# Row picks between the dense layers and the experts: merged branches laid out by token block, last ranks in the middle of the picks, loads and a store in another order

## The reference, cut to what matters

```python
merged = sigmoid(gate_a) * y_attn + sigmoid(gate_g) * y_gla     # T x D
h = h + (merged @ w_out) * valid
xn2 = rms_norm(h, norm2_w)
# hierarchical experts: best of 4 groups, then the best 2 of its 8 experts
y_ffn = hier_moe(xn2, router_group, router_expert, w_gate, w_up, w_down)
return h + y_ffn
```

## Time and profile before

| what | value |
|---|---|
| median of 3 runs | 678.75 us (676.87 to 681.87) |
| the profiled execution | 676.36 us, of which 674.5 us is the span from the first to the last instruction |
| busy share of the span | PE 97%, PEld 75%, DVE 58%, ACT 32%, POOL 15% |
| mean granted TensorE clock | 0.997 of full speed |
| experts (from 414.92 us on) | 38% of the span |

### The profile page before, as it was taken

How to read it: one execution, slowest core, us unless ns; L and a number is a source line. 1 busy time by engine, 2 the same in 40 slices (tenths; PEclk the granted TensorE clock), 3 DMA queues, 4 the chain that set the end, 5 groups by cost and what they waited for, 6 DMA issues and landing times.

```text
span 674.5 us, 11222 instructions
## 1 busy us (share of the span) xinstructions
PE 652.9 (97%) x4481; PEld 505.9 (75%) x4481; DVE 390.9 (58%) x736; ACT 216.2 (32%) x448; POOL 101.5 (15%) x138
## 2 busy tenths in 40 slices
PE   4999999999999999999999988999999999999998
PEld 2679999988888888888789987575757575656565
DVE  4648334778897878776663665453534435351515
ACT  5446222234434444432435455202020202110112
POOL 3300015999200000000000010110100101010010
PEclk9999999999999999999999999999999999999999
DMA  7442223202322211111554070999999999999973
GB/s 242 145 124 64 64 63 122 66 1 63 115 75 62 63 64 63 63 63 63 161 201 168 34 279 17 399 415 415 412 417 412 419 410 419 410 418 411 418 282 125
DMA packets 49798, 138.78 MB, mean 206 GB/s; under 512 B 6202, under 2 KB 28235, under 8 KB 41556
## 3 DMA queue, kind: packets, MB, share of 16 engines
q1 hardware_dynamic: 47298, 134.37, 52.3%
q0 software_dynamic: 2304, 3.64, 1.5%
q10 hardware_dynamic: 146, 0.07, 0.0%
HBM read 138.62 MB, written 4.19 MB: 212 GB/s over the span
## 4 chain that ended last, share of the span: by engine, by line
PE 87%; DVE 6%; ACT 4%; issue 2%; DMA 1%; POOL 0%; ACTq 0%; DVEq 0%
PE bank L960 17%; PE bank L603 12%; PE bank L604 12%; PE bank L605 12%; PE bank L973 8%; PE bank L1083 8%; PE bank L819 1%; DVE y_lo L1869 1%; PE bank L912 1%; PE bank L984 1%; PE bank L846 1%; PE bank L843 1%; PE bank L611 1%; ACT whi L1202 1%; DVE sig_a L1584 1%
## 5 line engine op out<-in xcount | busy, mean ns | idle before, releaser
L1515 DVE TENSOR_TENSOR wlo<-wraw,whi 128x2048 fp32r<-128x2048 f32 (+1 forms) x25 | 56.5, 2258 | 20.0 <-ACT whi L1202 20.0
L603 PE MATMUL bank<-xhi,whi 128*128 128x512 f32 x160 | 64.5, 403 | 0.0
L603 PE MATMUL bank<-whi,xhi 128*128 128x256 f32 x224 | 64.5, 288 | 0.0
L604 PE MATMUL bank<-xlo,whi 128*128 128x512 f32 x160 | 63.3, 396 | 0.0
L604 PE MATMUL bank<-wlo,xhi 128*128 128x256 f32 x224 | 63.0, 281 | 0.0
L605 PE MATMUL bank<-whi,xlo 128*128 128x256 f32 x224 | 62.9, 281 | 0.0
L605 PE MATMUL bank<-xhi,wlo 128*128 128x512 f32 x160 | 62.9, 393 | 0.0
L960 PE MATMUL bank<-wgate,xgT 128*64 128x256 f32 x512 | 58.4, 381 | 0.7 <-ACT xgT L1392 0.7
L960 PE MATMUL bank<-wup,xgT 128*64 128x256 f32 x512 | 58.4, 381 | 0.0
L973 PE MATMUL bank<-wdown,hT 128*64 128x512 f32 x256 | 58.1, 595 | 0.0
L1846 DVE SCALAR_TENSOR_TENSOR hg<-bank,pair_w,hs 128x256 f32<-128x256 f32 x16 | 7.7, 484 | 81.1 <-ACT hs L1420 81.1
(11 more groups left out here) (327 smaller groups left out, 1355.6 us busy)
## 6 DMA issues: line engine op xcount, KB each, us to landing
wgate<-in_expert_w_gate SPq DMA_DIRECT2D x32, 1024.0 KB, 13.8
wup<-in_expert_w_up SPq DMA_DIRECT2D x32, 1024.0 KB, 16.5
wdown<-in_expert_w_down SPq DMA_DIRECT2D x32, 1024.0 KB, 21.8
wraw<-in_w_in SPq DMA_DIRECT2D x17, 1024.0 KB, 5.5
wraw<-in_w_out SPq DMA_DIRECT2D x4, 1024.0 KB, 5.2
h<-in_x SPq DMA_DIRECT2D x4, 512.0 KB, 5.1
wraw<-in_w_gla_branch SPq DMA_DIRECT2D x2, 1024.0 KB, 5.0
wraw<-in_w_attn_branch SPq DMA_DIRECT2D x2, 1024.0 KB, 5.1
```

The lines of the kernel that those rows point to most:

```text
L603: nc.tensor.matmul(ps, lhi(k), rhi(k), start=(k == 0), stop=False)
L604: nc.tensor.matmul(ps, lhi(k), rlo(k), start=False, stop=False)
L1515: nc.vector.tensor_tensor(wl, raw, wh.bitcast(F32), ALU.subtract).then_inc(s_lo, 1)
```

## The change

`mhi` and `mlo` become `[P, NB, KT, P]`, block first, so that the 1024 values of a block and a partition lie in one run. `rowhi` and `rowlo` now read `h` in its own order and write one run; the step of 8 elements moves to the stationary operand of `select`. The merge (L1247, L1586) writes four pieces of 128 instead of one of 512; the products with `w_out` read 128 contiguous columns as before. `rowhi` and `rowlo` come one unit earlier in the list. `select` is split by part, and `rowhi`, `route`, `rank`, `pick`, `rowlo` of block 3 stand after the third of eight half selects. `weigh` 2 on DVE moves behind the copies of `xgT`, beside `weigh` 3. SP loads the three down weights before it stores the rows of block 3.

```diff
-        s += [("rowhi", (n - 6) // 4)] if n >= 6 and n % 4 == 2 else []
-        s += [("rowlo", (n - 7) // 4)] if n >= 7 and n % 4 == 3 else []
+        s += [("rowhi", (n - 5) // 4)] if n >= 5 and n % 4 == 1 else []
+        s += [("rowlo", (n - 6) // 4)] if n >= 6 and n % 4 == 2 else []
...
     s += [("rank", 2), ("hT", 15), ("pick", 2), ("rstd", 3), ("logit", 14), ("logit", 15)]
-    s += [("select", b) for b in range(3)] + [("route", 3), ("rowhi", 3), ("rank", 3), ("pick", 3), ("rowlo", 3), ("select", 3)]
+    s += [("select", 0, 0), ("select", 0, 1), ("select", 1, 0), ("rowhi", 3), ("route", 3), ("rank", 3), ("pick", 3), ("rowlo", 3)]
+    s += [("select", 1, 1), ("select", 2, 0), ("select", 2, 1), ("select", 3, 0), ("select", 3, 1)]
...
-        mhi = at("mhi", 48 * K1, [P, KT, T], F32R)
-        mlo = at("mlo", 64 * K1, [P, KT, T], F32R)
+        mhi = at("mhi", 48 * K1, [P, NB, KT, P], F32R)
+        mlo = at("mlo", 64 * K1, [P, NB, KT, P], F32R)
...
+        def rows_of(t, b):
+
+            return t[:, b, :, :].rearrange("p k c -> p (k c)")
...
-                    b = step[1]
-                    if b == 0:
+                    _, b, part = step
+                    if b == 0 and part == 0:
                         for k in PICK_BANKS:
                             pe.wait_ge(banks.free[k], banks.uses[k])
-                    for part, t in enumerate((mhi, mlo)):
-                        pe.wait_ge(s_rowlo if part else s_rowhi, b + 1)
-                        pe.wait_ge(s_ohr, b + 1)
-                        for g in range(4):
-                            for j in range(2):
-                                last = nc.tensor.matmul(tiles[PICK_BANKS[g]][:, j * 2 * P:(j + 1) * 2 * P],
-                                                        t[:, 2 * g + j, b * P:(b + 1) * P], onehot_r[:, b, :],
...
+                    pe.wait_ge(s_rowlo if part else s_rowhi, b + 1)
+                    pe.wait_ge(s_ohr, b + 1)
+                    for g in range(4):
+                        for j in range(2):
+                            rows = rows_of(mlo if part else mhi, b)[:, 2 * g + j:D:KT]
+                            last = nc.tensor.matmul(tiles[PICK_BANKS[g]][:, j * 2 * P:(j + 1) * 2 * P], rows, onehot_r[:, b, :],
...
             load(1, 1, True)
-            store_rows(NB - 1)
             sp.wait_ge(s_pick[3], 1)
             sp.wait_ge(s_cast, 2)
             load(0, 0, False, (1,))
             load(1, 1, False)
+            store_rows(NB - 1)
...
-                        nc.scalar.activation(mhi[:, j, :], sig_a[:, j, :], ACT.Copy).then_inc(s_mhi, 1)
+                        nc.scalar.activation(mhi[:, :, j, :], by_block(sig_a[:, j, :]), ACT.Copy).then_inc(s_mhi, 1)
...
-                    nc.scalar.activation(mhi[:, :, b * P:(b + 1) * P], by_chunk(b), ACT.Copy,
+                    nc.scalar.activation(rows_of(mhi, b), h[:, b, :], ACT.Copy,
                                          scale=b1[:, b, 5:6]).then_inc(s_rowhi, 1)
...
                 elif kind == "weigh":
-                    weigh(step[1])
+                    if step[1] < NB - 2:
+                        weigh(step[1])
...
-                    nc.vector.scalar_tensor_tensor(mlo[:, :, cb], by_chunk(b), b1[:, b, 5:6], mhi[:, :, cb].bitcast(F32),
+                    nc.vector.scalar_tensor_tensor(rows_of(mlo, b), h[:, b, :], b1[:, b, 5:6], rows_of(mhi, b).bitcast(F32),
                                                    ALU.mult, ALU.subtract).then_inc(s_rowlo, 1)
...
                 last.then_inc(s_xgT[2 * s], 1)
+            weigh(NB - 2)
             weigh(NB - 1)
```

More of the change, by code:

```diff
@@ L542, in split, with by_block @@
             return own if c == 0 else w_view(t[split_buffer(c)], c)
-        def by_chunk(b):
-            return h[:, b, :].rearrange("p (c k) -> p k c", k=KT)
+        def by_block(t):
+            return t.rearrange("p (b t) -> p b t", b=NB)
+        def rows_of(t, b):
+            return t[:, b, :, :].rearrange("p k c -> p (k c)")
         def q_heads(b, g):
@@ L618, in cols, with tokens @@
                 return lambda k: t[:, k, a:b]
+            def tokens(t, b):
+                return lambda k: t[:, b, k, :]
             def first_outputs():
@@ L630, in first_outputs @@
                             pe.wait_ge(s_mhi, k + 1)
-                            nc.tensor.matmul(ps[:, 0:CW], mhi[:, k, 0:P], wh[:, k, :], start=(k == 0), stop=False)
-                            nc.tensor.matmul(ps[:, 0:CW], mhi[:, k, 0:P], wl[:, k, :], start=False, stop=False)
+                            nc.tensor.matmul(ps[:, 0:CW], mhi[:, 0, k, :], wh[:, k, :], start=(k == 0), stop=False)
+                            nc.tensor.matmul(ps[:, 0:CW], mhi[:, 0, k, :], wl[:, k, :], start=False, stop=False)
                     for i, (ps, wh, wl) in enumerate(pair):
@@ L635, in first_outputs @@
                             pe.wait_ge(s_mlo, k + 1)
-                            last = nc.tensor.matmul(ps[:, 0:CW], mlo[:, k, 0:P], wh[:, k, :], start=False, stop=(k == KT - 1))
+                            last = nc.tensor.matmul(ps[:, 0:CW], mlo[:, 0, k, :], wh[:, k, :], start=False, stop=(k == KT - 1))
                         if ks[-1] == KT - 1:
@@ L710, in _ @@
                         ps = banks.take(pe, "unit", step)
-                        last = mm3(ps[:, 0:n], cols(mhi, u * P, (u + 1) * P), cols(mlo, u * P, (u + 1) * P),
+                        last = mm3(ps[:, 0:n], tokens(mhi, u), tokens(mlo, u),
                                    cols(wh, 0, n), cols(wl, 0, n), KT)
@@ L901, in _ @@
                 elif kind == "select":
-                    b = step[1]
-                    if b == 0:
+                    _, b, part = step
+                    if b == 0 and part == 0:
                         for k in PICK_BANKS:
                             pe.wait_ge(banks.free[k], banks.uses[k])
-                    for part, t in enumerate((mhi, mlo)):
-                        pe.wait_ge(s_rowlo if part else s_rowhi, b + 1)
-                        pe.wait_ge(s_ohr, b + 1)
-                        for g in range(4):
-                            for j in range(2):
-                                last = nc.tensor.matmul(tiles[PICK_BANKS[g]][:, j * 2 * P:(j + 1) * 2 * P],
-                                                        t[:, 2 * g + j, b * P:(b + 1) * P], onehot_r[:, b, :],
-                                                        start=(b == 0 and part == 0 and j == 0), stop=(b == NB - 1 and part == 1 and j == 1))
-                            if b == NB - 1 and part == 1:
-                                last.then_inc(s_pick[g], 1)
+                    pe.wait_ge(s_rowlo if part else s_rowhi, b + 1)
[4 more added lines that the diff above has]
+                            last = nc.tensor.matmul(tiles[PICK_BANKS[g]][:, j * 2 * P:(j + 1) * 2 * P], rows, onehot_r[:, b, :],
+                                                    start=(b == 0 and part == 0 and j == 0), stop=(b == NB - 1 and part == 1 and j == 1))
+                        if b == NB - 1 and part == 1:
+                            last.then_inc(s_pick[g], 1)
             def oh(s, b):
@@ L1585, in _ @@
                             dve.wait_ge(s_mhi, j + 1)
-                            nc.vector.tensor_tensor(mlo[:, j, :], t, mhi[:, j, :].bitcast(F32), ALU.subtract).then_inc(s_mlo, 1)
+                            nc.vector.tensor_tensor(mlo[:, :, j, :], by_block(t), mhi[:, :, j, :].bitcast(F32), ALU.subtract).then_inc(s_mlo, 1)
                     elif name == "wo":
@@ L1779, in _ @@
                     dve.wait_ge(s_rowhi, b + 1)
-                    cb = slice(b * P, (b + 1) * P)
-                    nc.vector.scalar_tensor_tensor(mlo[:, :, cb], by_chunk(b), b1[:, b, 5:6], mhi[:, :, cb].bitcast(F32),
+                    nc.vector.scalar_tensor_tensor(rows_of(mlo, b), h[:, b, :], b1[:, b, 5:6], rows_of(mhi, b).bitcast(F32),
                                                    ALU.mult, ALU.subtract).then_inc(s_rowlo, 1)
```

## The result

| kernel | median, us | runs | ratio to the kernel before, 95% interval |
|---|---|---|---|
| before | 677.27 | 16 | |
| changed | 681.43 | 16 | 1.0056 (1.004 to 1.0072) |

The change makes the kernel 0.56% slower, about 3.8 us by the ratio (4.2 between the medians). Forecast were 673.7 us, 5.0 less than 678.75, the median of three runs of the kernel before; the 16 runs here put that kernel at 677.27. The profiled execution of the changed kernel has a span of 679.5 us, 5.0 more than before.

The account below looks back on a forecast made before the run. PE was taken to bound the kernel, with its weak stretch before the experts. The order saves 5.0 us, the step, weighing and SP's order cost 0: 678.75 - 5.0 = 673.7 us, range 671.3 to 680.3.

Parts of the forecast that it names:

- The bound and the order: PE bounds; reordering picks and ranks around the selects moves the first expert product from 414.92 to 409.93, 5.0 us.
- The standstill of the earlier trace: PE idle about 2 us before hT 15, until 400.54; claimed to go, and by assumption the clock's fall with it.
- The splits: rowhi on ACT and rowlo on DVE, read and written in one run, fall to 1.05 and 1.28 us.
- The deferred weighing: weigh 2 and 3 behind DVE's copies: info ready at +5.94, PE there at +5.99 us, cost 0, at most 2.0.
- The stationary operand with a step: 64 fp32r select loads on PE with columns 32 bytes apart: taken as no extra cost, 0.119 us per product.
- p: Spacing in us between select products on PE, forecast 0.119.
- 402.15 + 64p: Start of the first expert product on PE's sum, p being the spacing of the 64 select products in us.
- The first rival: At the selects the step costs, spacing 0.22 us: first expert product at 416.2, total 680.0 us; chance 0.15.
- SP's order: Three down weights before block 3's store: cost 0, only a tail of 3 MB in front, late gathers harmless.
- Sum: Whole kernel: 5.0 us less than 678.75, giving 673.7 us, 0.74% less.
- The range: Whole kernel: 671.3 to 680.3 us, from PE's least sum less scatter up to the first rival.

Follow-up runs that it names:

- e4_run_loads_store: Changed kernel with the selects' stationary operands in one run and block 3's store again before the down weights: 674.53 us, ratio 0.9925 to the kernel before.
- e2_store_last: Kernel before with only SP's order changed, three down weights loaded before block 3's rows are stored: 680.29 us, ratio 1.0015.
- e3_run_loads: Changed kernel with the selects' stationary operands in one run again, the store still behind the down weights: 673.3 us, ratio 0.9918 to the kernel before.
- e8_weigh_early: e4_run_loads_store with block 2's weighing moved on DVE to just behind the remainder of block 3: 672.34 us, ratio 0.9929 to the kernel before.
- e11_e4_again: e4_run_loads_store run once more, unchanged: 671.96 us, ratio 0.9926 to the kernel before.
- e5_step2: Changed kernel with the store before the down weights and rows stored in runs of two, so select operands have step 2: 673.0 us, ratio 0.9933.
- e9_turned_step: e4_run_loads_store with the step of 8 put on the turned loads of gathered rows, ACT writing scaled rows in one run: 672.0 us, ratio 0.992.
- e7_layout_alone: Kernel before with only the new layout, short splits and stepped select operands; order and SP's queue untouched: 682.77 us, ratio 1.0072.
- e10_store_last_again: e3_run_loads run once more, unchanged: 673.18 us, ratio 0.9944 to the kernel before.

## Why the prediction was wrong

**The bound and the order: right.** The chain, link by link, gave 409.93 for the first expert product. With the step and the late store taken out (e4_run_loads_store) it is 410.15, and 409.85 in the second take; the time is 0.75% below the kernel before, where 5.0 us were forecast. The standstill of the earlier trace rows went, and none of the ten profiled executions in the new order, that of the changed kernel among them, shows a fall of the clock between 398 and 415.

The 5.0 us are two things, though. From the last product of rank 2 to the first expert product it is 16.50 us in the kernel before, 14.92 in e2_store_last, which has the same order but no fall of the clock there, and 11.4 to 11.6 in the new order without the step (e3_run_loads, e4_run_loads_store and their repeats). So 3.4 to 3.5 us come from the order itself and 1.6 from a fall that the profiled execution of before happened to have; the prediction took its going with the standstill as an assumption. How many executions of the kernel before have that fall isn't on record.

**The splits: right in the main.** L1388 (`rowhi`) took 1142 ns on the median and L1788 (`rowlo`) 1277 ns, against 1.05 and 1.28 us. Neither is on PE's path.

**The deferred weighing: a little off.** Forecast were 0 us with 0.05 to spare. In e4_run_loads_store `info` was ready 5.92 us after the last group's start (forecast 5.94), but PE had come 5.90 us after it (forecast 5.99), and it stands 0.42 us before L930. This is most of what its way from the first expert product to the end is longer than before (260.1 against 259.6 us). In the changed kernel PE waits for nothing there: its last group takes 1 us longer while DVE's copies start after the group's first products, so `info` is ready 6.33 us after the group's start and PE comes at 6.64. Moving it (e8_weigh_early) gained nothing.

**The stationary operand with a step: the term that failed.** The prediction took p = 0.119 us, with 0.22 as the upper bound, because stepped turned loads were 0.108 to 0.115 us apart and fp32r loads in a run 0.113 us. It read both as one rate of delivery, a column in 0.84 ns, that an fp32r load would not exceed. The runs show instead that the cost of the step goes by the kind of load: a step of 32 bytes adds 52 ns to a turned load of 141 ns and 150 ns to an fp32r load of 188 ns, and of the first 5 ns reach the distance between two products, of the second 123. Whether the 0.108 us of L662 has the price of its step in it already can't be said, as no row has it without the step. The prediction's estimate of 107 ns for a load of 128 columns fits the spacing of fp32r loads in one run, and not with the step of 8. The real p is 0.242 us; 64 x 0.123 = 7.9 us, and the formula of the prediction, 402.15 + 64p, gives 417.6, measured 417.83, of which 0.4 us is a later end of the dense stage. The first rival had the side right, that the step costs, with a chance of 0.15. No run shows its p of 0.22; the runs showed 0.234 at a step of 4 and 0.242 at 8. The splits' own rows, doubled by the same step, were the better neighbours than rows of PE with another kind of load.

**SP's order: the other term that failed.** Forecast 0, measured 2.0 us (681.43 less 679.39, and 261.6 less 259.8 us of span behind the first expert product). Two sentences failed. The first is that the store finds at most the tail of the 3 MB in front: it was issued 6.2 us behind the weights, as reckoned, but these filled the DMA engines only from about 419 on, and it landed 3.9 us later than with a free queue. The second is that a late gather for body 1 has most of a body to spare. It doesn't: before the change the second gather took 10.5 us from its issue to its landing, at 437.7, and the eight transposes that read it started at 439.7, 2.0 us later. A delay of 3.9 us of the store used all that up and 1.6 us of PE. The early weights brought nothing back; no reader of them had been waiting.

**Sum.** 5.0 won by the order and the clock (first L967 5.1 us earlier in e11_e4_again), 7.9 lost to the step, 2.0 to the store: +4.9 us, where the profiled spans show +5.0 (679.5 less 674.5) and the ratio of the runs +3.8. Most of what is between has a place. The profiled execution of before took 676.36 us, 0.9 less than the median of 677.27, and that of the changed kernel 681.29, 0.1 less than its median. A part of this, 0.4 us, shows already at the end of the dense stage (398.79 against 398.42 for the same rank product). Medians of one kernel moved by 2.6 us from one set of runs to the next (674.53 and 671.96 for e4_run_loads_store). The range, 671.3 to 680.3, missed 681.43, because it summed the step at 0.22 and the store at 0. That it came so near is luck in part: its base of 678.75 was 1.5 us above the median of 16 runs, and the same sum from 677.27 ends at 678.8.

The versions without the two failed parts beat both kernels: e4_run_loads_store, e5_step2 and e9_turned_step all lie 0.7 to 0.8% under the kernel before.

## What to carry to other kernels

When a step can't be avoided, it belongs where it is hidden: on a split under another engine's work, or on turned loads, and not on plain fp32r stationary operands that follow each other with 256 moving columns. Storing runs of two (step 2) gives both sides nearly all of their speed: loads of 194 instead of 188 ns, 1.27 us of ACT instead of 1.14, and 1.7 us of DVE in four pieces instead of 1.28 in one. A row of another kind of the same instruction is no bound: the same step reached the spacing with 5 ns in one kind and 123 ns in the other. Before a store is put behind loads on one queue, follow it to its last reader: here store, gather and transposes were one chain with 2 us of slack. And when a saving contains a fall of the clock, price it apart: it was 1.6 of 5.0 us here, and of three executions with a standstill at this place one did not have it.

## What the runs showed of the hardware

Fp32r stationary loads of 128 columns at the upper clock took 188 ns in one run, 194 ns at a step of 8 bytes, 330 ns at 16 and 338 ns at 32; products of 256 columns that follow each other were 0.113 to 0.119, 0.120, 0.234 and 0.242 us apart. Turned fp32 loads took 141 ns in one run and 193 ns at 32 bytes; a group of 16 with its matmuls took 1.97 and 2.05 us. Stepped fp32r products at the granted clock 0.50 were 0.24 us apart, as at 1.00; those in one run were 0.23 and 0.12. ACT wrote 1024 values in 2.25 us reading with a step of 32 bytes, in 1.14 us from a run. A 512 KB store issued 6.2 us after three loads of 1 MB on the same queue landed 6.99 us after its issue, and 3.1 us after it with none in front. Behind standstills of PE of 1.85 us (kernel before), 0.72 us (e7_layout_alone) and 1.76 us (e2_store_last, at 442) the granted clock was at 0.50 for a while; behind one of 1.82 us (e2_store_last, at 402) and waits of 1.3 to 1.6 us (changed kernel, e3_run_loads, e10_store_last_again) it stayed at 1.00.
